# Sums of the later modulation vectors moved from TensorE to GpSimd, and the gate projection split into single k-steps

## What is computed

```python
def first_block(x, c, norm_g, w_ada, b_ada, w_in, ...):
    mod = silu(c) @ w_ada + b_ada                    # 1024 x 3072
    shift, scale, gate = jnp.split(mod, 3, axis=-1)
    h = rms_norm(x, norm_g) * (1.0 + scale) + shift
    proj = h @ w_in
    ps = token_shift(proj[..., :D_SHIFT], mu_shift)  # r, k, v, g and two low-rank inputs
    y_r, g_r = rwkv7_mix(ps, ...)                    # y_r is multiplied by silu(g_r)
    ...
def second_block(x, c, ada_w, ada_b, ...):
    mod = silu(c) @ ada_w + ada_b                    # 1024 x 6144
    sh_m, sc_m, g_m, sh_f, sc_f, g_f = jnp.split(mod, 6, axis=-1)
    ...
```

## Time and profile before

| | us |
|---|---|
| median of three runs | 1393.48 (1389.54 to 1395.79) |
| the profiled execution, its own time | 1391.97 |
| span of the profiled execution | 1389.9 |
| busy: PE | 1292.5 (93%) |
| busy: DVE | 559.7 (40%) |
| busy: ACT | 351.2 (25%) |
| busy: POOL | 160.5 (12%) |

### The profile page before, as it was taken

One profiled execution on the slowest core, in us unless ns is written; L12 is line 12 of the kernel. 1 busy time (PEld: TensorE's weight loads), 2 busy tenths in 40 slices (PEclk: granted clock), 3 DMA queues, 4 the chain that ended last, 5 costly groups with the idle time before them and its releaser, 6 DMA issues.

```text
span 1389.9 us, 21101 instructions
## 1 busy us (share of the span) xinstructions
PE 1292.5 (93%) x7560; PEld 640.0 (46%) x7561; DVE 559.7 (40%) x1034; ACT 351.2 (25%) x759; POOL 160.5 (12%) x278
## 2 busy tenths in 40 slices
PE   5999999999999998999999998999999987897777
PEld 1445656568954444554445545433333333332222
DVE  1366363655214333349786635312212212121115
ACT  1223231422135442221467510101111101110102
POOL 4011010101120000000000001411121111111110
PEclk9999999999999999999999999999999999999999
DMA  9250704323163110014112384789999999999995
GB/s 365 84 212 11 279 26 167 138 79 149 35 187 147 46 46 1 0 49 167 52 57 76 122 348 182 276 350 396 411 412 419 399 406 421 403 402 416 409 391 209
DMA packets 40420, 303.93 MB, mean 219 GB/s; under 512 B 7964, under 2 KB 8116, under 8 KB 22800
## 3 DMA queue, kind: packets, MB, share of 16 engines
q1 hardware_dynamic: 31808, 285.12, 52.3%
q0 software_dynamic: 8528, 17.67, 4.1%
HBM read 299.49 MB, written 13.75 MB: 225 GB/s over the span
## 4 chain that ended last, share of the span: by engine, by line
PE 74%; DMA 14%; DVE 6%; issue 2%; ACT 2%; POOL 1%; DVEq 0%; SPq 0%; ACTq 0%; POOLq 0%
PE bank L858 21%; PE bank L2874 12%; DMA arena<-in_w_down 11%; PE bank L790 8%; PE bank L2892 7%; PE bank L904 4%; PE bank L969 2%; PE bank L847 2%; PE bank L2862 2%; DMA arena<-in_ada_w 1%; PE bank L1186 1%; PE bank L1130 1%; PE bank L1107 1%; PE bank L893 1%; PE bank L2883 1%
## 5 line engine op out<-in xcount | busy, mean ns | idle before, releaser
L858 PE MATMUL bank<-hT,arena 128*128 128x512 f32 x720 | 320.0, 599 | 0.0
L2874 PE MATMUL bank<-arena,hT 128*64 128x512 f32 x1024 | 231.9, 603 | 18.0 <-DMA arena<-in_w_gu 17.6
L858 PEld LDWEIGHTS bank<-hT,arena 128*128 128x128 f32 x720 | 135.0, 191 | 162.6 <-issue 159.2
L2874 PEld LDWEIGHTS bank<-arena,hT 128*64 128x64 f32 x1024 | 72.9, 138 | 156.3 <-issue 138.1
L2892 PE MATMUL bank<-arena,yT 128*64 128x512 f32 x512 | 123.8, 628 | 15.7 <-DMA arena<-in_w_down 13.9
L790 PE MATMUL bank<-arena,yT 128*128 128x512 f32 x256 | 114.5, 601 | 2.4 <-DVE yT L1685 2.3
L3062 DVE TENSOR_SCALAR hT<-hT 128x256 f32<-128x256 f32 x32 | 9.4, 295 | 248.4 <-ACT hT L3000 248.4
L3000 ACT ACTIVATE hT<-bank 128x256 f32<-128x256 f32 x32 | 12.3, 384 | 264.0 <-PE bank L2874 264.0
L790 PEld LDWEIGHTS bank<-arena,yT 128*128 128x128 f32 x256 | 48.1, 192 | 60.0 <-issue 56.2
L2892 PEld LDWEIGHTS bank<-arena,yT 128*64 128x64 f32 x512 | 36.1, 143 | 78.7 <-issue 61.2
L904 PEld LDWEIGHTS bank<-arena 64*64 64x64 f32 x1856 | 59.3, 135 | 23.8 <-issue 14.4
(11 more groups left out here) (489 smaller groups left out, 1609.1 us busy)
## 6 DMA issues: line engine op xcount, KB each, us to landing
arena<-in_w_gu SPq DMA_DIRECT2D x63, 2048.0 KB, 26.8
arena<-in_w_down SPq DMA_DIRECT2D x32, 2048.0 KB, 30.5
arena<-in_w_in SPq DMA_DIRECT2D x53, 512.0 KB, 4.6
arena<-in_ada_w SPq DMA_DIRECT2D x24, 1024.0 KB, 5.1
arena<-in_w_ada SPq DMA_DIRECT2D x8, 1024.0 KB, 9.1
arena<-in_w_out SPq DMA_DIRECT2D x8, 1024.0 KB, 9.0
arena<-in_w_ada SPq DMA_DIRECT2D x8, 512.0 KB, 4.7
arena<-expert_rows SPq DMA_DIRECT2D x4, 1024.0 KB, 8.4
```

The lines of the kernel that those rows point to most:

```text
L858: last = T.matmul(bank[0:rows, :], w[:, k, 0:rows], hT[:, k, :], start=k == 0, stop=k == KD - 1)
L2874: last = T.matmul(banks[1 + ub][MT * h:MT * h + MT, :], tile.xT[:, k, :], wgu[u][:, k // 4, k % 4, :, 256 * h:256 * h + 256], start=k == 0 ...
```

## The change

Three things change.

1. The sums of groups 2, 3 and 4 leave PE. POOL makes them: for each k the tile is multiplied in place by one value of silu(c) per partition (128 x 2048) and added to `mod_sum` (128 x 2048, in SBUF). For each group these are eight multiplications and seven additions: k = 0 stands ahead of the mask of level 3, k = 1 ahead of that of level 4, k = 2 ahead of that of level 5, and k = 3 to 7 behind `mod_io`. The eight values of silu(c) that a partition holds are taken one by one, so the sum over partitions is still to be made: four products with a block of ones (`mod_rows`, PE) in the next pair, and DVE adds the bias (`mod_made`).
2. The gate projection (g) of pair p is no longer made whole at l = 4 of the pair before. Its eight k-steps (`gate_steps`) stand in pair p itself, at l = 4, l = 5 and the six later places of the old `ada_step`. In pair 3 they stand two by two at l = 1 to 4, ahead of the value rows. The token shift of the gate moves to the end of the pair, its exponential and clamp into the next pair.
3. Ahead of pair 0 the key norm and the decays are put before the projection and the shift of v, and the whole projection of g goes out of that stretch; the eight steps of group 1 follow each other.

```diff
@@ SP: the order of the loads
-        ada_after = {("proj", 0, 3): KD + 1, ("proj", 1, 3): KD, ("proj", 2, 3): KD, ("proj", 3, 3): KD - 1}
+        ada_after = {("proj", 0, 2): KD}
+        for p in range(PAIRS - 1):
+            then = [("proj", p + 2, j) for j in PROJ_ORDER[:3]] if p + 2 < PAIRS else [("va", 0), ("proj", PAIRS - 1, 3), ("va", 1)]
+            for name, count in zip([("proj", p, 3)] + then, (3, 1, 2, 2)):
+                ada_after[name] = ada_after.get(name, 0) + count
@@ POOL
+            def mod_part(g, k):
+
+                n = KD * g + k
+                slot, turn = ada_slot(n)
+                c = cact[:, KD + k:KD + k + 1]
+                eng.wait_ge(ada_sem[slot], 16 * (turn + 1))
+                if k:
+                    done(G.tensor_scalar(ada_slots[slot], ada_slots[slot], c, None, MUL))
+                    done(G.tensor_tensor(mod_sum, mod_sum, ada_slots[slot], ADD))
+                else:
+                    if g > 2:
+                        eng.wait_ge(filled, fill_at[("mod", g - 1)] + 1)
+                    done(G.tensor_scalar(mod_sum, ada_slots[slot], c, None, MUL))
+                eng.sem_inc(s_ada_used, 1)
...
                     if l > 2:
+                        if p + 1 < PAIRS:
+                            mod_part(2 + p, l - 3)
                         eng.wait_ge(filled, fill_at[("W", p, l - 2)] + 1)
...
                 mod_io(1 + p)
+                if p + 1 < PAIRS:
+                    for k in range(LEVELS - 4, KD):
+                        mod_part(2 + p, k)
@@ PE
             lora(0)
+            key_norm(0)
             pe_proj(("proj", 0, 2))
-            key_norm(0)
             eng.wait_ge(s_first_in, 1)
-            for k in range(3):
-                pe_ada(1, k)
-            pe_proj(("proj", 0, 3))
-            for k in range(3, KD):
+            for k in range(KD):
                 pe_ada(1, k)
...
+                def gate_steps(count):
+
+                    name = ("proj", p, 3)
+                    if not p and not gate_k[0]:
+                        eng.wait_ge(s_mod, 2)
+                    w = chunk_ready(name)
+                    for _ in range(count):
+                        k = gate_k[0]
+                        gate_k[0] += 1
+                        bank = fill(name) if k == KD - 1 else begin(name)
+                        last = T.matmul(bank[:, :], w[:, k, :], hT[:, k, :], start=k == 0, stop=k == KD - 1)
+                        if k == KD - 1:
+                            full(last)
+
+                def mod_rows(g):
+
+                    eng.wait_ge(s_ada_used, KD * (g + 1))
+                    bank = fill(("mod", g))
+                    for j in range(4):
+                        last = T.matmul(bank[32 * j:32 * j + 32, :], ones[:, 0:32], mod_sum[:, 512 * j:512 * j + 512],
+                                        start=True, stop=True)
+                    full(last)
...
                 if p:
                     mean(p - 1)
-                if not q:
-                    eng.wait_ge(s_mod, 5)
-                ada_step()
+                    mod_rows(1 + p)
                 va_rows(1)
...
-                    if l <= 4 and q:
+                    if l <= 3 and q:
                         pe_proj(("proj", q, PROJ_ORDER[l - 1]))
-                    elif q and l == LEVELS - 2:
-                        ada_step()
+                    elif q:
+                        gate_steps(1)
                     else:
+                        if l <= 4:
+                            gate_steps(2)
                         va_rows(2 if l <= 4 else 1)
@@ ACT, ahead of pair 0
             lora_exp(0)
+            decay_sigmoid(0)
+            key_norm(0)
             proj_raw(0, 2)
-            decay_sigmoid(0)
-            proj_raw(0, 3)
-            key_norm(0)
             decay_exp(0)
@@ DVE
             decay_clamp(0)
+            key_norm_in(0)
+            decays(0)
+            bonus_in(0)
             proj_shift(0, 2)
-            decays(0)
-            key_norm_in(0)
-            bonus_in(0)
-            proj_shift(0, 3)
             operands(0)
...
                 if p:
+                    gate_clamp(p - 1)
                     center(p - 1)
+                    mod_made(1 + p)
                 level_add(p, 1)
...
                 level_add(p, 4)
-                if q:
-                    proj_shift(q, 3)
+                if not q:
+                    proj_shift(p, 3)
...
-                eng.wait_ge(s_yg, p + 1)
-                dve_clamp(("gate", p), t_g)
                 if q:
-                    dve_ada(2 + p)
+                    proj_shift(p, 3)
+                else:
+                    gate_clamp(p)
```

More of the change, by code:

```diff
@@ L161, in plan, with plan_on @@
             fills.append((name, by))
+        def plan_on(name, by, bank):
+            held[name] = bank
+            plan(name, by)
+            free_banks[0].remove(bank)
         def plan_proj(p, j):
@@ L198, in build_program @@
                 plan(("W", p, l), "act")
-                if l <= 4 and q:
+                if l <= 3 and q:
                     plan_proj(q, PROJ_ORDER[l - 1])
+                if l == 4 and not q:
+                    plan_on(("proj", p, 3), "act", ADA_BANK)
+                    free_banks[0].append(ADA_BANK)
                 if l in (2, 4) and not q:
@@ L1271, in out_norm, with gate_exp @@
                 eng.sem_inc(s_rn, 1)
+            def gate_exp(p):
+                if p + 1 < PAIRS:
+                    eng.wait_ge(s_ops, 3 * (p + 1) + 1)
+                eng.wait_ge(s_shift, ITEM[p, 3] + 1)
+                act.done(S.activation(t_g, gsh[:, p % 2, :], ACT.Exp, scale=-1.0))
+                eng.sem_inc(s_yg, 1)
             proj_raw(0, 1)
@@ L1303, in act_block1 @@
                     if l == 1 and p:
+                        act_sigmoid(("gate", p - 1), (t_g, None))
                         out_square(p - 1)
@@ L1306, in act_block1 @@
                         key_square(q)
-                    if l <= 4 and q:
+                    if l <= 3 and q:
                         proj_raw(q, l - 1)
+                    if l == 4 and not q:
+                        proj_raw(p, 3)
                     if l in (2, 4) and not q:
@@ L1330, in act_block1 @@
                 if q:
-                    eng.wait_ge(s_ops, 3 * q + 1)
-                act.done(S.activation(t_g, gsh[:, p % 2, :], ACT.Exp, scale=-1.0))
-                eng.sem_inc(s_yg, 1)
+                    proj_raw(p, 3)
+                else:
+                    gate_exp(p)
                 bank = take(S, ("Y", p))
@@ L1399, in act_block1 @@
                     act_sigmoid(("agate", p + 1), (aegs[:, (p + 1) % 2, :], None))
+        items = [(0, n) for n in range(3)]
+        for p in range(PAIRS - 1):
+            items += [(p + 1, n) for n in range(3)] + [(p, 3)]
+        items.append((PAIRS - 1, 3))
+        ITEM = {name: n + 1 for n, name in enumerate(items)}
         squares = [("key", 0)]
@@ L1538, in pair_out, with gate_clamp @@
                 eng.sem_inc(s_pair, 1)
+            def gate_clamp(p):
+                eng.wait_ge(s_yg, p + 1)
+                dve_clamp(("gate", p), t_g)
             shift(("wa",), 0, TW, col("mu_shift", 16))
@@ L1748, in build_program @@
         side = sb("side", [P, 2176])
+        mod_sum = side[:, 0:2048]
         mask16 = sb("mask16", [P, 2 * P], mybir.dt.bfloat16)
```

65 lines of the change are left out of this document (40 added, 25 removed).

## The result

The changed kernel takes 1503.97 us (median of four runs, 1501.88 to 1509.49) where the kernel before takes 1393.92 (1389.54 to 1395.79, four runs): ratio 1.080, interval 1.0775 to 1.0824, 8% slower. The profiled execution took 1504.03 us, with a span of 1502.3.

The account below looks back on a forecast made before the run. PE looked like the bound, in a ping-pong with ACT and DVE whose gaps it fills. 1391.97 - 8.4 - 1.5 + 8.0 - 4 + 7.7 + 86.1 + 6 = 1486 us; range 1415 to 1540.

Parts of the forecast that it names:

- Turns and exclusion: POOL and DVE instructions with two SBUF inputs exclude each other for a whole instruction, and whoever waited goes next.
- The sign that was named: DVE's bonus and operands, L1588 to L1602, each several us long, right behind the end of a POOL instruction.
- the second rival: DVE's back-to-back instructions go first, POOL holds it up to 8 us a pair: 1410 us, chance 7%.
- Price of a multiplication, 2.0 us: POOL's multiplication over 2048 elements holds what DVE wants for 2.0 us, from a copy's rate; ends 0 and 6.2.
- The fourth rival: The multiplication is dear: at 4.5 us each 1531 us in all, at 6.2 us 1562; chance 16%.
- The third: Rival: the multiplication excludes nobody, only additions hold DVE, 17 us a pair: 1446 us, chance 19%.
- k = 3 to 7, 28.7 us a pair: Ten POOL instructions behind `mod_io`, 32.6 us, all ahead of `level_add(4)`; less overlaps 28.7 a pair, 86.1 for three.
- k = 1 at nothing, k = 2 at 7.7 in three pairs: k = 1 falls beside DVE's PSUM work, no cost; k = 2 delays `level_add(2)` by 3.1, 3.1 and 1.5 us.
- Level 4, -8.4, and fillers, -1.5: One k-step replaces the projection, so `level_add(4)` comes 2.8 us earlier, three times; shorter fillers elsewhere gain 1.5 in all.
- Clock, 6: PE, idle some 20 us ahead of `level_add(4)`, then runs at half clock: 2 us a pair, 6 in all.
- Pair 3, +8.0: PE is nearly always busy there, so eight k-steps (7.0 us) and `mod_rows` (1.0) are added whole.
- Ahead of pair 0, -4: The gate's projection, 7.13 us, leaves this stretch; gain of 4 us, between 1 and 8.

Follow-up runs that it names:

- experiments 1 to 5: Changed kernel with POOL's sums left out (1393.24 us), additions alone (1449.24), all in quarters (1477.58), additions alone moved later (1409.78); kernel before with POOL's reads added (1488.55).
- the quarters: Changed kernel with each POOL multiplication and addition cut into four over 512 elements: 1477.58 us; with additions alone, so cut, 1440.66 us.
- without sums: Changed kernel with POOL's multiplications and additions for k = 1 to 7 left out, waits and tiles kept: 1393.24 us.
- Experiment 3: Kernel before, with POOL given the same multiplications and additions on a scratch tile: 1488.55 us; with memsets of about the same time instead: 1430.12 us.

## Why the prediction was right, and where its sizes were off

The forecast was 1486 us, and 1504 came, inside the range; the mechanism is the forecast one, shown by experiments 1 to 5. By its own steps:

- **Turns and exclusion**: right for instructions with two SBUF inputs, and shown by the quarters. "For a whole instruction" holds for additions only. The sign that was named, L1588 to L1602 each several us long, came for four of the nine (4.08 to 4.87 us, pair 1); of the others L1596, L1597 and L1602 passed at full speed in the tail of a multiplication, L1600 right at the start of one, and L1588 took 1.24. Two in a row were named as a sign of the second rival; they are seen beside multiplications only. Not seen in the rows: a DVE TENSOR_SCALAR from SBUF is held by the whole multiplication (the first of the two clamps, 5.44 of their 10.06 us, to 115.5), and a DVE instruction that has just begun can be held through several of POOL's.
- **Price of a multiplication, 2.0 us**: wrong. It lasts 5.6 and holds DVE's two-input instructions some 3.5 us. The rate read from the 192 elements of the earlier trace rows (6.2 us for 2048) was nearer than the copy's rate, which I had preferred because the DVE instruction beside it was late by only 0.08 us. The fourth rival had the right duration, but counted it whole. The third was also added up wrong: by its own terms it is 22.5 - 3.9 = 18.6 us a pair and not 17, and the additions alone did cost 19.2.
- **k = 3 to 7, 28.7 us a pair**: between the sums of levels 2 and 4, 44.4 us (234.27 to 278.70), against 21.3 before (196.10 to 217.44) and 18.7 without sums (188.41 to 207.14): 25.7 by POOL. Two errors of opposite sign: only seven of the ten instructions come ahead of `level_add(4)`, since two or three of DVE's pass in the tail of each multiplication; but the four multiplications among them hold 3.5 us, not 2.0. 4 x 3.5 + 3 x 4.6 = 27.8, less what overlaps. I had 10 of them and 32.6. That 28.7 came so near to 25.7 is luck.
- **k = 1 at nothing, k = 2 at 7.7 in three pairs**: the worst term. From the first mask to `level_add(2)` it is 34.2 us in pair 1 instead of 25.5, and in pair 0 9.6 more than before: 27 us in three pairs, 19 more than forecast. Two multiplications more than twice as long as assumed push POOL's queue by 7 us, so that k = 1 no longer falls beside the gram masks but beside the shift and `pair_out`, and k = 2 beside the clamps. The price of the cover wasn't carried from one item of POOL's queue to the next.
- **Level 4, -8.4, and fillers, -1.5**: without sums the pairs take 77.5, 79.0 and 78.3 us, together 3.7 less than before, not 9.9. `level_add(4)` does come 2.6 us earlier within the pair (44.2 after the first mask instead of 46.8). But PE, which had worked without a gap, has now waited, and the products behind the next 32 run at half clock (0.50 granted from 211.0 to 214.5). PE without sums, pair 1:

```profile
207.93 1.15 PE L948 MATMUL bank<-arena 64*64 64x64 f32 x32 [2.66 <-issue]
209.01 1.95 PE L1024 MATMUL bank<-hT,arena 128*128 128x512 f32 x2
210.89 3.67 PE L948 MATMUL bank<-arena 64*64 64x64 f32 x48
```

  The 48 small passes took 2.07 us in the earlier trace rows and take 3.67; from `level_add(4)` to the next pair it is 34.9 us instead of 33.0. So 1.9 of the 2.6 us won are given back; the rows at half clock are the likely cause, and no run separates them from the rest of that stretch. I had counted half clock for the long stall only.
- **Clock, 6**: in the changed kernel the stretch behind `level_add(4)` is 33.4 us, 0.4 more than before. The half clock shows earlier: behind idle times of 7.64 and 10.29 us the 32 small products take 1.97 us instead of 1.15, and the projection at 236.97 takes 8.02 instead of 7.13.
- **Pair 3, +8.0**: right for the work (70.7 us once the wait was gone), 14.8 measured. The step left out was that the gate's sum needs a bank which DVE has to empty first; two parts of the change share it.
- **Ahead of pair 0, -4**: -4.7.
- **The rest of the program**: taken as unchanged, +3.5 here; it varies between 996 and 1002 us in the kernels that make the sums whole, and I have no cause for it.

On the exclusion the Trainium skill, "SBUF — State Buffer", Who interferes with whom, says that a DVE instruction with two SBUF inputs contends with a GpSimd instruction that reads SBUF and not with one that only writes, while the 2-port modes contend with both (an exception that the prediction's sentence on one SBUF input left out). Experiment 3 agrees with each (0.69 us beside memsets, 2.84 for the two clamps). That the pair is locked "for the whole instruction" holds for the addition and not for the multiplication against two-input instructions, and that the order of issue decides doesn't tell of the turns: here the measurement goes ahead. "GPSIMD Engine Reference", Engine selection, with its "roughly line-rate" for one input, gives the estimate of 1.7 us that stands in the prediction; the traces show 5.44.

## What to carry to other kernels

An engine with much idle time isn't free if it shares a port with one on the critical path: the same 21 additions cost 58 us beside DVE's SBUF work and 14 behind most of it. Before work goes to POOL, lay its instructions one after another beside DVE's, carrying each delay to the next, and ask of each DVE instruction whether it reads two operands from SBUF, or is a TENSOR_SCALAR or a copy from SBUF to SBUF (one clamp took 4.08 us at 205.44 beside a multiplication, instead of 0.43); and see first whether DVE can do the work itself in a wait (2.35 us here instead of 5.6 + 4.6). A bank or a buffer that two parts of a change share is a wait between them.

## What the runs showed of the hardware that was not expected

- POOL's TENSOR_SCALAR over 128 x 2048 float32, with a value for each partition, lasts 5.44 us undisturbed, longer than the TENSOR_TENSOR with two inputs (4.5). In quarters four of them take 6.18.
- Turns by whole instructions are the rule, but a DVE instruction begun 0.3 to 0.5 us ahead of four additions in a row was passed over by all four, in each of three pairs. Ahead of four multiplications it wasn't, in two.
- Two executions whose DVE reached the port 1.7 us apart in pair 0 took 99.9 and 113.5 us for it. 1.6 of the 1.7 us were PE's clock: behind the same wait of 2.93 us 1.00 was granted once and 0.53 once.
- PE's granted clock fell to 0.50 for 3.5 us and more behind a gap of 2.66 us in a stretch that was otherwise nearly full, in each of three pairs; in the kernel before, without the gap, it stayed at 1.00 there.
